# Differential attention: both exponentials of a query tile ahead of the second copy of the transposed probabilities

## What is computed

```python
def block(qb):
    sc = jnp.einsum('bqhcd,bkhcd->bhcqk', qb, k, preferred_element_type=f32) * scale
    p = jax.nn.softmax(sc, axis=-1)
    p = p[:, :, 0] - lam * p[:, :, 1]
    return jnp.einsum('bhqk,bkhd->bqhd', p.astype(v.dtype), v)
```

## Time and profile before

| what | value |
|---|---|
| runs | 3405.02, 3408.56 (median), 3410.43 us |
| the profiled execution's own time | 3410.63 us |
| its span in the trace | 3408.9 us, of 40159 instructions |
| PE, matmuls busy | 2869.9 us (84%) |
| DVE busy | 1775.7 us (52%) |
| ACT busy | 1213.5 us (36%) |
| POOL busy | 887.4 us (26%) |
| 56 tiles of DA's first seven heads | from about 1847 to 2429.5 us |
| the 8 tiles of its last head | from 2429.5 to about 2490 us |

### The profile page before, as it was taken

How to read it: one execution, slowest core, us unless ns; L and a number is a source line. 1 busy time by engine, 2 the same in 40 slices (tenths; PEclk the granted TensorE clock), 3 DMA queues, 4 the chain that set the end, 5 groups by cost and what they waited for, 6 DMA issues and landing times. The chain is left out here.

```text
span 3408.9 us, 40159 instructions
## 1 busy us (share of the span) xinstructions
PE 2869.9 (84%) x14648; PEld 2317.6 (68%) x14648; DVE 1775.7 (52%) x1969; ACT 1213.5 (36%) x1825; POOL 887.4 (26%) x460
## 2 busy tenths in 40 slices
PE   6989888597877887775928999999886988999987
PEld 5777777375656676654816777777665776787875
DVE  5454348626656446666873665666644114444444
ACT  3122221314434233434043555555622214443331
POOL 3453342131222322121304333333212222000011
PEclk9999999798988898887959999999987999999998
DMA  3000006210000100001611111111022110000011
GB/s 112 32 31 18 31 25 221 105 41 21 18 25 18 37 25 25 18 18 37 228 63 50 38 38 38 38 38 38 25 75 74 44 43 19 13 6 12 6 62 67
DMA packets 45691, 159.77 MB, mean 47 GB/s; under 512 B 5793, under 2 KB 7073, under 8 KB 45601
## 3 DMA queue, kind: packets, MB, share of 16 engines
q1 hardware_dynamic: 38688, 133.32, 11.8%
q10 hardware_dynamic: 6912, 25.17, 2.1%
HBM read 133.30 MB, written 16.78 MB: 44 GB/s over the span
## 5 line engine op out<-in xcount | busy, mean ns | idle before, releaser
L108 POOL TENSOR_SCALAR w_hi<-w_raw 128x1024 fp32r<-128x1024 f32 x156 | 177.7, 1139 | 1987.5 <-PE pj L134 674.7
L132 PE MATMUL pj<-x_hi,w_hi 128*128 128x512 f32 x1132 | 453.4, 401 | 63.5 <-PEq L580 24.7
L133 PE MATMUL pj<-x_lo,w_hi 128*128 128x512 f32 x1132 | 445.8, 394 | 0.0
L134 PE MATMUL pj<-x_hi,w_lo 128*128 128x512 f32 x1132 | 445.1, 393 | 0.0
L110 POOL TENSOR_TENSOR w_lo<-w_raw,w_hi 128x1024 fp32r<-128x1024 f32 x156 | 399.3, 2559 | 23.4 <-issue 11.3
L950 PE MATMUL pj<-x_hi,w_hi 128*128 128x512 f32 x704 | 312.5, 444 | 42.9 <-DVEq L1166 35.2
L132 PEld LDWEIGHTS pj<-x_hi,w_hi 128*128 128x128 f32 x1132 | 216.3, 191 | 114.0 <-issue 65.5
L951 PE MATMUL pj<-x_lo,w_hi 128*128 128x512 f32 x704 | 291.5, 414 | 0.0
L952 PE MATMUL pj<-x_hi,w_lo 128*128 128x512 f32 x704 | 290.0, 412 | 0.0
L1413 PE MATMUL pj<-x_hi,w_hi 128*128 128x512 f32 x512 | 224.2, 438 | 34.8 <-DVEq L1620 26.2
L133 PEld LDWEIGHTS pj<-x_lo,w_hi 128*128 128x128 f32 x1132 | 216.0, 191 | 45.4 <-issue 1.7
(11 more groups left out here) (335 smaller groups left out, 5734.7 us busy)
## 6 DMA issues: line engine op xcount, KB each, us to landing
w_raw<-w_slots SPq DMA_DIRECT2D x158, 512.0 KB, 3.5
out_ada_rows<-ada_t ACTq DMA_DIRECT2D x48, 512.0 KB, 4.8
x_res<-o_t SPq DMA_DIRECT2D x12, 1024.0 KB, 4.0
o_t<-x_res SPq DMA_DIRECT2D x12, 1024.0 KB, 5.5
o_t<-x_t SPq DMA_DIRECT2D x8, 1024.0 KB, 11.4
da_swapped<-da_raw SPq DMA_DIRECT2D x64, 128.0 KB, 2.3
out_t<-o_t SPq DMA_DIRECT2D x4, 1024.0 KB, 4.4
out_c<-c_in SPq DMA_DIRECT2D x2, 512.0 KB, 3.4
```

The source lines that it names most:

```text
L108: nc.gpsimd.tensor_scalar(g.w_hi[:, u, :], g.w_raw[:, u, :], 1.0, 0.0, ALU.mult, ALU.add)
L132: nc.tensor.matmul(dst, w_hi, x_hi[:, k, cols], start=(j == 0), stop=False)
L133: nc.tensor.matmul(dst, w_hi, x_lo[:, k, cols], start=False, stop=False)
L134: mm = nc.tensor.matmul(dst, w_lo, x_hi[:, k, cols], start=False, stop=(j == n - 1))
```

## The change

In ACT's list the second copy of the transposed probabilities of tile n now stands behind the exponential of map 1 of tile n + 1, instead of ahead of it. Nothing else changes, and the lists of PE, DVE, POOL and SP are the same.

```diff
@@ -1591,9 +1591,9 @@
                     take_p(h, n, 0)
                     if nxt:
                         exp(*nxt, 0)
-                    take_p(h, n, 1)
                     if nxt:
                         exp(*nxt, 1)
+                    take_p(h, n, 1)
                     if n in (4, 5) and not last:
                         high(h + 1, 1 - u, n - 4)
                     if n == 3:
```

## The result

The changed kernel takes 3445.01 us (median; 3440.69 to 3451.69) against 3407.1 us of the kernel before (3405.02 to 3410.43): a ratio of 1.0112, 95% interval 1.0093 to 1.0132. It is 37.9 us slower, where 45.5 were forecast.

A forecast was written before the change was run, and what follows sets the result against it. PE was taken to bound the first seven heads, with ACT waits in every last-head tile. 34.1 + 6.5 + 4.9 = 45.5 us on the profiled 3410.63, less 2.1 for the median: 3454.1 us, range 3440 to 3470.

The forecast's parts named there:

- first seven heads: PE waits at the product for ACT's later copy in 49 of 56 tiles: 34.1 us more.
- of it the seven tiles ahead of the wait for DVE: Beside q's rotary embedding, PE waits for DVE's `combine` anyway, so the delay costs 0, bounds 0 and -0.3.
- last head, the ring: Last head's cycle from maxima through copy, product and scores takes in map 1's exponential: 1.15 us in six tiles, 6.5 in all.
- last head, the clock: PE's clock falls to half in four of six last-head tiles instead of one: 3 x 1.62 = 4.9 us.
- The price of a tile: First seven heads: 0.63 us of waiting plus 0.09 of unhidden weight load, 0.72 per tile; 0.63 where spacing is wider.
- the bound of 16: Upper bound of the last head's clock term: five tiles with product and scores at half speed, 16 us.
- rival (e): Clock falls in the first seven heads too: 78 us more, 3532 us; chance 0.04 with others above 3470.
- Rival (a): No further fall of the clock in the last head: 34.1 + 6.5, 3449.2 us; chance 0.20.
- Rival (b): The product's weights are loaded during PE's wait: 0.09 us less in 49 tiles, 3449.7 us; chance 0.04.
- Rival (c): PE makes the delay good in its "issue" idle places around the scores: 3409 to 3415 us; 0.04 with (f).
- Rival (d): Faster: the earlier second exponential closes PE's "issue" idleness ahead of the scores, 24.0 us: 3385 us; chance 0.02.
- Rival (f): PE does not feel ACT's order, because the transposes release the copy, not ACT's list; chance 0.04 with (c).

The follow-up runs named there:

- e2: The changed kernel's new order kept in the first seven heads only, the last head in the old order; 3435.9 us, ratio 1.0079 to the kernel before.
- e5: Kernel before, with the new order only in tile 2 of each of the first seven heads; 3408.4 us in one run, against 3407.0.
- e9: Kernel before, ACT order untouched, with useless matmuls in PE's waits in tiles 1 to 7 of the last head; 3403.1 us, ratio 0.9982.
- e4: Changed kernel, with useless matmuls where PE waits for ACT in tiles 1 to 7 of the last head; 3437.8 us, ratio 1.0084 to the kernel before.
- e7: Kernel before, with three small copies ahead of ACT's second copy in the first seven heads; 3410.2 us in one run, against 3407.0.
- e8: Kernel before, with eight small copies ahead of ACT's second copy in the first seven heads; 3419.4 us in one run, against 3407.0.
- e3: Changed kernel, with each tile's last two projection k-steps ahead of the product in the first seven heads; 3425.0 us, ratio 1.0043 to the kernel before.
- e6: Kernel before, with the new order only in tile 1 of each of the first seven heads; 3417.9 us in one run, against 3407.0.

## Why the prediction was right, and where its sizes were not

The account, from the first product to the 64th in the two traces (635.8 before, 674.2 after): 38.4 us more. Outside of it DA begins 3.9 us sooner in the trace of the changed kernel and what follows is 2.0 us shorter, so its whole span is only 32.5 us longer. The 2.0 us are the 64th product and the matmuls behind it, which ran at the full clock in the trace after and at the lower level in that of before (16 loads in 1.86 against 3.49 us). The start of DA lies between 1845 and 1854 us in the traces of this study; this is a difference in the stages ahead, which are the same in all kernels, and its cause was not looked into.

| term | forecast | measured | from |
|---|---|---|---|
| first seven heads | 34.1 | 22.6 | trace after; e2: 23.0 |
| of it the seven tiles ahead of the wait for DVE | 0 | 0 | e5 |
| last head, the ring | 6.5 | 6.1 | e9 against e4, less 0.55 of e4's matmuls |
| last head, the clock | 4.9 | 9.7 | after less e4 up to the 63rd product (11.3), less 1.6 of before |
| sum | 45.5 | 38.4 | 38.4 in the traces |

The first term came out 11.5 us too high and the last 4.8 too low. That the total is only 7 us off is therefore in part luck; the direction, the waits and the places are not.

**What bounds the kernel, and the direction**: right. PE had no slack in the first seven heads, the exponential had 3.3 us and the copy about 0.3. By e7 and e8 the copy may start 1.40 us behind the exponential of map 0 without loss and not 1.93 us behind it (1.26 before), and e3 shows that nothing else costs more than 1.2 us in all.

**The price of a tile** was mis-sized. The wait itself was right: 0.63 us forecast, 0.56 to 0.65 in the trace. The term added to it had the wrong sign. I took 1.99 us from a product behind a wait in the last head and 1.90 from one without a wait in the middle, and read the difference, 0.09, as a load that isn't hidden. But the one is followed by the scores and the other by a projection. Like with like it is 1.78 against 1.90 ahead of the projection (after, before) and 1.99 against 2.10 ahead of the scores (before's last head, e3): a product behind a wait is 0.12 us *shorter*. Its first matmul starts with its first load, while behind a running matmul the first load stands 0.23 us ahead. The matmuls themselves show it, the product's and the next work's, before and after:

```profile
1996.28 1.95 PE L1459 MATMUL pj<-da_p_t,da_v 128*128 128x128 f32 x16
...
1997.98 0.47 PE L1413 MATMUL pj<-x_hi,w_hi 128*128 128x512 f32 x1
```

```profile
2008.46 2.05 PE L1459 MATMUL pj<-da_p_t,da_v 128*128 128x128 f32 x16 [0.20 <-ACT da_p_t L1555]
...
2010.27 0.48 PE L1413 MATMUL pj<-x_hi,w_hi 128*128 128x512 f32 x1
```

From matmul to matmul the product is 0.11 us *longer* behind a wait (1.81 against 1.70), so the load does show, as I had said. But I had counted the delay from load to load, 0.63 us, and the first 0.23 of it delay no matmul: 0.63 - 0.23 + 0.11 = 0.51 us per tile, and not 0.72. Against 0.72 that is 0.21 us less, in 49 tiles 10.3 us, and 34.1 - 10.3 = 23.8, near to the 22.6 measured (0.47 us in each of the 48 distances that are longer).

**The seven tiles beside the rotary embedding**: right, and for the reason given (e5, e6). `combine` did start earlier (its first instruction 3.59 us ahead of POOL's addition instead of 2.93) and did not end earlier: its last step still takes 3.26 us and ends 1.09 us behind POOL's addition.

```profile
2043.88 2.65 POOL L1382 TENSOR_TENSOR da_raw<-da_raw,da_swapped 128x1024 f32<-128x1024 f32 x1
2044.36 3.26 DVE L1684 SCALAR_TENSOR_TENSOR da_p<-da_p_second,da_rden,da_p 128x1024 f32<-128x1024 f32 x1
2047.67 0.42 PEld L1449 LDWEIGHTS pj<-ident,da_p 128*128 128x128 f32 x4 [0.70 <-DVE da_p L1684]
```

**The last head**: the ring within 0.4 us; six distances cost 6.6 us where 6.9 were forecast, and the seventh and the last tile together give back 0.5 where it was 0.4. For the clock I had taken three further tiles of 1.62 us; five of the seven distances from product to product were longer than in e4, by 1.6 to 2.6 us each, since the lower level often lasted into the scores; 11.3 us in all, 9.7 more than the 1.6 of before. The mechanism was right (e4) and the bound of 16 held.

**The clock in the first seven heads** stayed at 1.00 with 0.6 us of waiting in each tile, as forecast; rival (e) is out. Rival (a), no further fall, is out by e4, though its total of 3449.2 is nearer to the result than the forecast's 3454.1: the two errors of the forecast had opposite signs. Rival (b) would have the load done during the wait; the load is the row that waits, [0.64 <-ACT], so its mechanism is out, and its figure of 3449.7 is still too high. By the rule that it cites from the Trainium skill ("TensorE: Matmul & The Clock Gate", Step-by-step: what each phase is for), PE pulls loads ahead of running matmuls; here no load is pulled over a semaphore that it waits for: the product's first load and its first matmul start together, at 2008.46. Rival (c) is out: the idle places marked "issue" are the same after as before, 24.0 and 19.9 us in 55 tiles each, so they are no backlog that a pause lets PE work off. Rival (d) is out: the second exponential was done 4 us ahead of the scores and nothing came of it. Rival (f) is out: the copy did move behind the exponential, and PE felt it.

## What to carry to other kernels

Before moving work ahead on a shared engine, read for each of the two instructions who waits for it and when that engine gets there: here one had 3.3 us to spare and the other 0.3, and the engine behind it had no slack at all. A delay was lost in full (e6) unless the next wait of the delayed engine ended by something that the delay had not moved; then it cost nothing (e5, where 0.5 us met a wait of 1.17). When two durations are compared, the instruction before and the one behind must be of the same kind in both.

## What was not expected of the hardware

- A group of 16 weight loads and matmuls is 0.12 us shorter from its first load when PE has waited just before it (1.78 against 1.90 us, 1.99 against 2.10), and 0.11 us longer from its first matmul (1.81 against 1.70).
- From the product to matmuls over 64 rows there is a step of 0.2 us more than to matmuls over 128 rows (2.10 against 1.90). What makes the step was not tested.
- Useless matmuls in PE's waits paid for themselves: the clock stayed at 1.00 where it was 0.78, and the last head of the changed kernel went from 71.0 to 59.6 us.
